# Squares of the residual shared by two engines, an earlier scaling in stick-breaking, and latent heads stacked by parity

## The chip, the core and the metric

The program runs on one core of a Trainium2 chip. It is one launch that computes two transformer layers in float32. The metric is the device time of the launch in microseconds, lower is better. The engines are named as the profile names them: PE is TensorE (matmuls; PEld its weight loads), DVE is VectorE, ACT is ScalarE, POOL is GpSimd, SP is SyncE, which here only issues DMAs. Times and starts in rows are microseconds from the start of the profiled span.

## What is computed

512 tokens, width 1024, two layers. Layer 0 mixes by eight latent heads (MLA: a query of 64 plain and 32 rotary rows per head, one rotary key shared by all heads) and eight block-attention heads (MoBA); layer 1 mixes by sixteen stick-breaking heads. Each mixing and each feed-forward part ends in a norm and is added to the residual h, and the next part starts with the norm of the new h.

```python
def mla_attention(...):                       # layer 0, heads 0..7
    q = rmsnorm(c_q) @ w_uq                   # per head: 64 plain rows, 32 rotary rows
    kv = rmsnorm(c_kv) @ w_ukv                # per head: 64 key rows, 64 value rows
    logits = (q_nope . k_nope + rope(q_rope) . rope(k_rope)) * scale   # causal softmax
def stick_breaking_attention(q, k, v):        # layer 1, 16 heads
    z = q . k * scale
    log_1m = where(strict, log_sigmoid(-z), 0)
    acc = reverse_cumsum(log_1m) - log_1m
    w = where(strict, exp(log_sigmoid(z) + acc), 0)
    return w . v
for layer in range(2):
    mixed = attention(rmsnorm(h)) @ w_out
    h = h + rmsnorm(mixed, mix_post_g)
    f = (silu(gate) * up) @ w_down            # gate, up = rmsnorm(h) @ w_gate_up
    h = h + rmsnorm(f, ffn_post_g)
```

## The kernel before

Everything is held transposed: a tile has 128 rows of the model width and 512 tokens as columns. To keep float32 accuracy each operand is split into a high part (rounded by a copy on ACT) and a low part (the difference, on DVE), and each product is three matmuls, hi x hi, lo x hi and hi x lo (`mm3`, lines 381 to 383). Weights stream through three slots of `w_raw` in chunks of 128 x 1024: SP loads a chunk when the low part of the chunk three before is done, ACT writes `w_hi` (`split_hi`, L369), DVE writes `w_lo` (`split_lo`, L376), PE uses it. The order on every engine is written out by hand; an engine takes its instructions strictly in that order and waits on semaphores, so a DVE instruction that waits holds up all that stand behind it.

**The three residual steps** (`res_dve`, `res_act`, `res_pool`, after each mixing or feed-forward part but the last) run in two halves of 256 tokens. For each of eight row tiles n, DVE writes the scaled branch to a quarter of `tf` (L647), POOL adds it to the residual (L725), ACT writes `u_hi` (L691), DVE writes `u_lo` (L657), and PE multiplies with the first three chunks of the next part, `c`, `c+1`, `c+2` (`first_products`). The splits of these chunks stand between the `u_lo` steps: the one of `c+1` behind tile 2 of the first half. Then the new h is squared on ACT (L482, two halves of eight tiles) and summed on DVE (L488, 14 adds of 128 x 256 into `sq_sum`, half after half). PE sums over rows (`stat_pe`, L411), ACT and DVE make 1/rms (L432, L437, L442), PE spreads it over the rows (`spread_pe`, L424), DVE copies it to `r_pre` (L449).

**The start of stick-breaking** (L2073 to L2093 on DVE). Projections of the pairs of heads are scaled by `r_pre` as they leave their PSUM banks (`sb_scale`, L1490), q and k of a pair are split (L1500, L1504), v is transposed on PE (L1434) and split (L1510). PE makes z for a head (`z_pe`), ACT and DVE make the softplus (`z_act_exp`, `z_dve_clamp` L1544, `z_act_ln`, `z_dve` L1555), DVE splits it (L1563, L1567), PE sums it (`c_pe`, L1579), ACT makes the stick weights (L1588), DVE and POOL split them (L1595, L1599), PE multiplies with v. The z of a pair's second head uses banks 3 to 5, in which the projections (0,2), (1,0) and (1,1) lie until DVE has scaled them. The banks' reads are counted by `qj_read`; bank 7 is used by all later projections in turn.

**The latent heads** (`layer0_items`, `item_pe`, `item_scale`, `scores_pe`). For each pair of heads PE projects q of head 0, k of head 0, q of head 1, k of head 1 and both values; a query tile has 96 rows, its last 32 are rotated on DVE and POOL (L1096, L1104, L1107, L1111), then q and k are split (ACT L1239, DVE L1286) and the scores are made with 96 contracted rows.

## Time and profile before

| | us |
|---|---|
| median of 3 runs | 1394.21 (1387.27 to 1395.02) |
| the profiled execution, its own time | 1389.55 |
| its span | 1387.5 |
| PE busy in it | 1333.9 |

The page gives busy time by engine and the chain of work that ended last; the waits view says which instruction of another engine ended an engine's idle time; the timeline gives the instructions of one engine in order of time, with the idle time ahead of each in brackets; the windows view gives busy time and the granted TensorE clock in a stretch (1.00 is 2.4 GHz, 0.50 is 1.2 GHz). The chain of waits is PE for 88% of the span, so what counts is PE's idle time, its clock, and the work that it has.

### The profile page before, as it was taken

What the parts mean: (1) busy time and instruction counts of PE and PEld (TensorE: products, weight loads), DVE (VectorE), ACT (ScalarE), POOL (GpSimd) and SP (SyncE); (2) the same over time, 40 slices, a digit from 0 to 9 for tenths busy, and PEclk for the clock granted to TensorE, in tenths of its full rate; (3) what the DMA queues carried; (4) which work ended last, traced back from release to release, by engine and by line L of the source; (5) the groups of instructions that cost most, each with busy time, mean ns of one, the idle gap of its engine ahead of it and who ended that gap; (6) DMA issues with size and microseconds to landing.
All of it is one profiled execution on the core that took longest, in us unless ns stands there. A gap on an engine that the chain in (4) does not pass through costs nothing.

```text
span 1387.5 us, 17888 instructions
## 1 busy us (share of the span) xinstructions
PE 1333.9 (96%) x6687; PEld 1122.3 (81%) x6687; DVE 730.9 (53%) x1005; ACT 543.7 (39%) x869; POOL 252.6 (18%) x185
## 2 busy tenths in 40 slices
PE   7888999999999999999988999999999999999997
PEld 5666888888888888888877888888898888888886
DVE  4777554437554544322467666765475455443223
ACT  5366665555322222222353444433553232232122
POOL 0333100033211111010231222222421111110002
PEclk9989999999999999999998999999999999999999
DMA  5311332132333333323221121120323333332321
GB/s 164 109 41 45 84 84 62 46 92 77 107 91 99 97 91 102 94 87 97 76 61 31 47 60 45 45 71 21 91 77 106 91 105 91 95 117 83 100 91 61
DMA packets 187219, 112.16 MB, mean 81 GB/s; under 512 B 8944, under 2 KB 181557, under 8 KB 187166
## 3 DMA queue, kind: packets, MB, share of 16 engines
q1 hardware_dynamic: 185356, 106.68, 26.3%
q0 software_dynamic: 640, 2.10, 0.5%
q10 hardware_dynamic: 1170, 2.66, 0.5%
q8 instruction: 35, 0.57, 0.2%
q14 instruction: 18, 0.15, 0.0%
HBM read 109.30 MB, written 4.74 MB: 82 GB/s over the span
## 4 chain that ended last, share of the span: by engine, by line
PE 88%; DVE 6%; ACT 2%; POOL 1%; issue 1%; DMA 1%; SPq 0%; POOLq 0%; DVEq 0%; ACTq 0%
PE banks L381 28%; PE banks L383 27%; PE banks L382 27%; PE banks L1579 3%; DVE w_lo L376 1%; PE banks L1373 1%; PE banks L424 1%; DVE u_lo L657 1%; DMA x_tokens<-in_x_dram 1%; ACT probsT_hi L1381 0%; DVE logits L1335 0%; PE banks L411 0%; DVE tf L1260 0%; DVE tf L647 0%; POOL rope_tmp L1104 0%
## 5 line engine op out<-in xcount | busy, mean ns | idle before, releaser
L381 PE MATMUL banks<-u_hi,w_hi 128*128 128x512 f32 (+1 forms) x1112 | 428.1, 385 | 10.0 <-DVE u_lo L657 6.5
L376 DVE TENSOR_TENSOR w_lo<-w_raw,w_hi 128x1024 fp32r<-128x1024 f32 (+2 forms) x200 | 291.9, 1463 | 272.1 <-ACT w_hi L369 271.8
L382 PE MATMUL banks<-u_lo,w_hi 128*128 128x512 f32 (+1 forms) x1112 | 421.5, 379 | 0.0
L383 PE MATMUL banks<-u_hi,w_lo 128*128 128x512 f32 (+1 forms) x1112 | 421.4, 379 | 0.0
L369 ACT ACTIVATE w_hi<-w_raw 128x1024 fp32r<-128x1024 f32 (+2 forms) x200 | 206.3, 1032 | 246.0 <-PE banks L383 246.0
L381 PEld LDWEIGHTS banks<-u_hi,w_hi 128*128 128x128 f32 x1112 | 213.0, 192 | 50.0 <-DVE u_lo L657 7.7
L383 PEld LDWEIGHTS banks<-u_hi,w_lo 128*128 128x128 f32 x1112 | 212.5, 191 | 38.9
L382 PEld LDWEIGHTS banks<-u_lo,w_hi 128*128 128x128 f32 x1112 | 212.7, 191 | 37.8 <-issue 1.0
L853 POOL TENSOR_TENSOR up<-up,gate 128x512 f32<-128x512 f32 x44 | 71.8, 1633 | 393.5 <-DVE up L877 358.5
L834 ACT ACTIVATE gate<-gate 128x512 f32<-128x512 f32 x44 | 27.9, 635 | 204.3 <-DVE gate L873 204.3
L1599 POOL TENSOR_TENSOR stick_lo<-stick,stick_hi 128x1280 fp32r<-128x1280 f32 x16 | 56.8, 3547 | 199.8 <-DVE stick_hi L1595 199.8
L381 PE MATMUL banks<-hidden_hi,w_hi 128*128 128x512 f32 (+1 forms) x198 | 73.6, 372 | 0.0
L383 PE MATMUL banks<-hidden_hi,w_lo 128*128 128x512 f32 (+1 forms) x198 | 73.4, 371 | 0.0
L382 PE MATMUL banks<-hidden_lo,w_hi 128*128 128x512 f32 (+1 forms) x198 | 73.4, 370 | 0.0
L381 PE MATMUL banks<-w_hi,hidden_hi 128*128 128x512 f32 x176 | 70.3, 399 | 0.4 <-ACT h_tokens L1044 0.3
L383 PE MATMUL banks<-w_hi,hidden_lo 128*128 128x512 f32 x176 | 69.4, 395 | 0.0
L382 PE MATMUL banks<-w_lo,hidden_hi 128*128 128x512 f32 x176 | 69.0, 392 | 0.0
L877 DVE TENSOR_TENSOR up<-banks,r_pre 128x512 f32<-128x512 f32 x44 | 30.4, 691 | 71.1 <-PE banks L383 71.1
L873 DVE TENSOR_TENSOR gate<-banks,r_pre 128x512 f32<-128x512 f32 x44 | 30.4, 691 | 69.8 <-PE banks L383 69.7
L1346 ACT ACTIVATE logits<-logits,neg_max 128x512 f32<-128x512 f32 (+1 forms) x64 | 35.3, 554 | 38.5 <-DVE neg_max L1339 38.5
L550 POOL TENSOR_TENSOR sq_sum<-sq_sum,sq_tile 128x512 f32<-128x512 f32 x14 | 18.2, 1300 | 174.6 <-ACT block_out L531 174.6
L725 POOL TENSOR_TENSOR residual<-residual,tf 128x256 f32<-128x256 f32 x42 | 41.5, 1019 | 33.9 <-DVE tf L647 33.9
(238 smaller groups left out, 2045.2 us busy)
## 6 DMA issues: line engine op xcount, KB each, us to landing
w_raw<-in_ffn_w_gate_up_dram SPq DMA_DIRECT2D x88, 512.0 KB, 3.7
w_raw<-in_ffn_w_down_dram SPq DMA_DIRECT2D x30, 512.0 KB, 3.5
w_raw<-in_sb_w_qkv_dram SPq DMA_DIRECT2D x24, 512.0 KB, 3.8
w_raw<-in_ab_w_in_dram SPq DMA_DIRECT2D x17, 512.0 KB, 3.9
w_raw<-in_ffn_w_down_dram SPq DMA_DIRECT2D x16, 448.0 KB, 3.4
w_raw<-in_ab_w_out_dram SPq DMA_DIRECT2D x8, 512.0 KB, 3.7
w_raw<-in_sb_w_out_dram SPq DMA_DIRECT2D x8, 512.0 KB, 3.7
bias_by_distance<-bias_rows ACTq DMA_DIRECT2D x1, 2560.0 KB
```

What stands on the lines that cost most here:

```text
L369: act.activation(wh[:, c.slot, 0:w], raw[:, c.slot, 0:w], ACT.Copy).then_inc(w_hi, 1)
L376: dve.tensor_tensor(wl[:, c.slot, 0:w], raw[:, c.slot, 0:w], wh[:, c.slot, 0:w].bitcast(F32), ALU.subtract).then_inc(w_lo, 1)
L381: nc.tensor.matmul(o, lh, rh, start=start, stop=False, skip_group_check=True)
L382: nc.tensor.matmul(o, lh, rl, start=False, stop=False, skip_group_check=True)
L383: return nc.tensor.matmul(o, ll, rh, start=False, stop=stop, skip_group_check=True)
L725: nc.gpsimd.tensor_tensor(hT[:, n, half(h)], hT[:, n, half(h)], quarter(n), ALU.add)\
L853: nc.gpsimd.tensor_tensor(us[:, n0 % 3, :], us[:, n0 % 3, :], gs[:, n0 % 3, :], ALU.mult)\
L873: nc.vector.tensor_tensor(gs[:, b, :], bank(2 * b), r_pre[:, :], ALU.mult).then_inc(gu_read, 1)
L877: nc.vector.tensor_tensor(us[:, b, :], bank(2 * b + 1), r_pre[:, :], ALU.mult).then_inc(gu_read, 1)
L1346: ins = act.activation(logits[:, b, at:at + w], logits[:, b, at:at + w], ACT.Exp, bias=nmx[:, b, i:i + 1], accum_out=den[:, b, i:i + 1])
L1579: mm = nc.tensor.matmul(Z[:, at:at + w], lt[:, :], n[:, COL_AT[jj]:COL_AT[jj] + w], start=False, stop=False, skip_group_check=True)
L1599: nc.gpsimd.tensor_tensor(swl[:, e, :], wf[:, :], swh[:, e, :].bitcast(F32), ALU.subtract)\
```

## The change

**Residual.** The sum of squares is shared: POOL adds the first half's seven tiles (after its residual adds), DVE the second half's; ACT squares the two halves in turn, tile by tile, and each half has two quarters of `tf` to itself. The split of chunk `c+1` on DVE comes behind tile 3 in place of tile 2. The split of `c+5` leaves the end of the residual step and comes behind `diag` and ahead of the copy to `r_pre` (on ACT behind the load of the function table). In layer 1's start PE makes the row sums inside the projection (1,0), behind its fifth row tile, where they came behind the whole of it, and the spread inside (1,1) behind its first row tile, where it came behind the fourth.

**Stick-breaking ramp.** DVE scales (1,0) and (1,1) before the clamp of head 0 and before the split of v; (1,1) goes to `diag`, since `tf` has two tiles. PE's z of head 1 waits for five bank reads in place of six. In the first pair DVE scales (1,2) ahead of two weight splits, which it used to follow.

**Latent heads.** k of both heads of a pair is one projection of 128 rows, and is split by two copies on ACT and two on DVE, one for each 64 rows. q of an odd head is a tile of 128 rows: its rotary rows are rows 32 to 63, its plain rows 64 to 127, and rows 0 to 31 hold other values that meet key rows of zero. q of an even head keeps its 96 rows above 32 rows of zero. The scores contract 128 rows. So the chunk of w_uq comes by three DMAs in place of one, the rotary table by two in place of one, the rotated key is written to both row ranges (one more POOL add at the first rotation), and POOL clears six pads at the start. The query tiles have two buffers in place of three.

```diff
@@ layer0_items
-                       ("mq", p, 1, cq, False, True), ("mk", p, 1, ck, False, False),
-                       ("mv", p, 0, ck, False, True), ("vt", p, 0, None, False, False)])
+                       ("mq", p, 1, cq, False, True), ("mv", p, 0, ck, False, True),
+                       ("vt", p, 0, None, False, False)])
@@ square_h, add_h_squares
-                before = (KD - 1) * h + n - 4
-                if before > 0:
-                    act.wait_ge(hq_added, H_ADDS * r + before)
-                dst = quarter((KD - 1) * h + n)
+                if n > 2:
+                    act.wait_ge((ha_added, hb_added)[h], (KD - 1) * r + n - 2)
+                dst = quarter(2 * h + n % 2)
...
-            nc.vector.tensor_tensor(acc[:, half(h)], acc[:, half(h)], quarter((KD - 1) * h + n), ALU.add)\
-                .then_inc(hq_added, 1)
+            op(acc[:, half(h)], acc[:, half(h)], quarter(2 * h + n % 2), ALU.add).then_inc(added, 1)
@@ res_dve
-                    if h == 0 and n == 2:
+                    if h == 0 and n == 3:
                         split_lo(dve, Chunk(c + 1))
...
-            for n in range(1, 4):
-                add_h_squares(dve, r, 0, n)
+            for n in range(1, 3):
+                add_h_squares(dve, nc.vector.tensor_tensor, r, 1, n)
             split_lo(dve, Chunk(c + 3))
-            for n in range(4, KD):
-                add_h_squares(dve, r, 0, n)
-            for n in range(1, KD):
-                add_h_squares(dve, r, 1, n)
+            for n in range(3, KD):
+                add_h_squares(dve, nc.vector.tensor_tensor, r, 1, n)
             split_lo(dve, Chunk(c + 4))
-            split_lo(dve, Chunk(c + 5))
@@ res_pool
+            for n in range(1, KD):
+                add_h_squares(pool, nc.gpsimd.tensor_tensor, r, 0, n)
@@ item_pe, item_act, item_lo
-                mm = project(pe, b[0:MLA_QH, :], c, KQ, 2 * MLA_QH, e * MLA_QH, MLA_QH, cqh, cql)
+                m = P if e else MLA_QH
+                mm = project(pe, b[0:m, :], c, KQ, 2 * MLA_QH, e * HD, m, cqh, cql)
             elif kind == "mk":
-                mm = project(pe, b[0:HD, :], c, KKV, P, e * HD, HD, ckh, ckl)
+                mm = project(pe, b, c, KKV, P, 0, P, ckh, ckl)
...
+                for rows, b in mk_dst(p):
+                    ins = act.activation(mq[2][rows, b, :], scaled_tile(it)[rows, :], ACT.Copy)
...
+                for rows, b in mk_dst(p):
+                    ins = nc.vector.tensor_tensor(mq[3][rows, b, :], scaled_tile(it)[rows, :],
+                                                  mq[2][rows, b, :].bitcast(F32), ALU.subtract)
@@ sb_pair_pe, sb_pair_dve
             if first:
-                pe.wait_ge(qj_read, 6)
+                pe.wait_ge(qj_read, 5)
...
+                if first:
+                    sb_scale(dve, p + 1, q, 2)
                 sb_split_dve(dve, p + 1, 1)
                 sb_split_dve(dve, p + 1, 2)
-                sb_scale(dve, p + 1, q, 2)
+                if not first:
+                    sb_scale(dve, p + 1, q, 2)
@@ vector, start of layer 1
-            stat_dve(dve, N_SB, 0, r_pre)
+            stat_dve(dve, N_SB, 0, None)
+            split_lo(dve, Chunk(CH_SB + 5))
+            stat_copy_dve(dve, N_SB, 0, r_pre)
...
             sb_scale(dve, 0, 0, 2)
+            sb_scale(dve, 1, 1, 0)
+            sb_scale(dve, 1, 1, 1)
             z_dve_clamp(dve, 0, 0)
             sb_item_dve(dve, 0, 0, 3)
-            sb_scale(dve, 1, 1, 0)
-            sb_scale(dve, 1, 1, 1)
@@ tensor, start of layer 1
-            sb_item_pe(pe, 1, 1, 0)
-            stat_pe(pe, N_SB, 0, (hq_added, 2 * H_ADDS))
-            sb_item_pe(pe, 1, 1, 1, lambda: spread_pe(pe, N_SB, 0))
+            def sums():
+                h_added(pe, 1)
+                stat_pe(pe, N_SB, 0, None)
+            sb_item_pe(pe, 1, 1, 0, sums, 4)
+            sb_item_pe(pe, 1, 1, 1, lambda: spread_pe(pe, N_SB, 0), 0)
```

DVE in the first half of the residual step ahead of layer 1 (`tf` is the scaled branch, `u_lo` the low part that PE waits for, `w_lo` the split of chunk `c+1`), before:

```order
L657 SCALAR_TENSOR_TENSOR u_lo<-residual,gains,u_hi 128x256
L647 SCALAR_TENSOR_TENSOR tf<-block_out,gains,banks 128x256
L376 TENSOR_TENSOR w_lo<-w_raw,w_hi 128x1024
L657 SCALAR_TENSOR_TENSOR u_lo<-residual,gains,u_hi 128x256
L647 SCALAR_TENSOR_TENSOR tf<-block_out,gains,banks 128x256
```

and now:

```order
L668 SCALAR_TENSOR_TENSOR u_lo<-residual,gains,u_hi 128x256
L658 SCALAR_TENSOR_TENSOR tf<-block_out,gains,banks 128x256
L668 SCALAR_TENSOR_TENSOR u_lo<-residual,gains,u_hi 128x256
L658 SCALAR_TENSOR_TENSOR tf<-block_out,gains,banks 128x256
L383 TENSOR_TENSOR w_lo<-w_raw,w_hi 128x1024
```

The first row of each is tile 2; tile 3 now stands ahead of the split. The other two residual steps move in the same way.

DVE at the start of layer 1, from the copy of the spread norm on (`softplus` 128x1280 is the clamp of head 0, then its log step; `tf` and `diag` are scaled projections), before:

```order
L449 COPY r_pre<-banks 128x512
L1490 SCALAR_TENSOR_TENSOR tf<-banks,r_pre 128x512 x2
L1500 TENSOR_TENSOR sb_q_lo<-tf,sb_q_hi 64x512 x2
L1504 TENSOR_TENSOR sb_k_lo<-tf,sb_k_hi 128x512
L1490 SCALAR_TENSOR_TENSOR tf<-banks,r_pre 128x512
L1544 TENSOR_SCALAR softplus<-softplus 128x1280
L1510 TENSOR_TENSOR sb_v_lo<-banks,sb_v_hi 128x4x64 x2
L1490 SCALAR_TENSOR_TENSOR tf<-banks,r_pre 128x512 x2
L1555 SCALAR_TENSOR_TENSOR softplus<-softplus,banks 128x1280
```

and now:

```order
L383 TENSOR_TENSOR w_lo<-w_raw,w_hi 128x1024
L462 COPY r_pre<-banks 128x512
L1537 SCALAR_TENSOR_TENSOR tf<-banks,r_pre 128x512 x2
L1547 TENSOR_TENSOR sb_q_lo<-tf,sb_q_hi 64x512 x2
L1551 TENSOR_TENSOR sb_k_lo<-tf,sb_k_hi 128x512
L1537 SCALAR_TENSOR_TENSOR tf<-banks,r_pre 128x512 x2
L1537 SCALAR_TENSOR_TENSOR diag<-banks,r_pre 128x512
L1591 TENSOR_SCALAR softplus<-softplus 128x1280
L1557 TENSOR_TENSOR sb_v_lo<-banks,sb_v_hi 128x4x64 x2
L1602 SCALAR_TENSOR_TENSOR softplus<-softplus,banks 128x1280
```

The scalings of (1,0) and (1,1) moved from behind the split of v to ahead of the clamp, and the split of `c+5` stands ahead of the copy.

POOL around the end of the same residual step, before:

```order
L725 TENSOR_TENSOR residual<-residual,tf 128x256 x14
L1834 MEMSET sb_v_hi 128x8x64
L1834 MEMSET sb_v_lo 128x8x64
L1839 MEMSET sb_q_hi 64x2x512 x2
L1839 MEMSET sb_q_lo 64x2x512 x2
```

and now:

```order
L729 TENSOR_TENSOR residual<-residual,tf 128x256 x14
L501 TENSOR_TENSOR sq_sum<-sq_sum,tf 128x256 x7
L1898 MEMSET sb_v_hi 128x8x64
L1898 MEMSET sb_v_lo 128x8x64
L1903 MEMSET sb_q_hi 64x2x512 x2
L1903 MEMSET sb_q_lo 64x2x512 x2
```

Seven adds stand ahead of the clears of the stick-breaking pads.

## Rows read from the trace of the kernel before

**Rows 1.** The page: busy us, share of the span and instructions by engine.
```profile
PE 1333.9 (96%) x6687; PEld 1122.3 (81%) x6687; DVE 730.9 (53%) x1005; ACT 543.7 (39%) x869; POOL 252.6 (18%) x185
```

**Rows 2.** Waits of PE: us in total, times, longest us.
```profile
PE banks L381 <- DVE mla_k_lo L1286: 9.0, 8, 2.7
PE banks L381 <- DVE u_lo L657: 6.5, 6, 1.9
```

**Rows 3.** Windows: busy us (x) of PE, PEld, DVE, ACT, POOL; PEclk, DMA, GB/s.
```profile
690.00:695.00 5.00, 5.00 (x25) 4.91 (x24) 2.83 (x6) 1.44 (x3) 0.00 (x0) 0.50 0.08 19
730.00:735.00 5.00, 5.00 (x18) 4.44 (x19) 4.89 (x6) 1.91 (x3) 0.00 (x0) 0.50 0.00 0
1006.50:1012.50 6.00, 6.00 (x28) 6.00 (x29) 3.68 (x9) 2.18 (x5) 1.37 (x2) 0.50 0.32 91
315.00:320.00 5.00, 5.00 (x31) 5.00 (x31) 3.77 (x9) 2.02 (x5) 1.21 (x2) 0.66 0.37 107
```

**Rows 4.** Timeline of DVE, third residual step: start us, us, instruction, [idle before].
```profile
1003.30 0.57 DVE L657 SCALAR_TENSOR_TENSOR u_lo<-residual,gains,u_hi 128x256 fp32r<-128x256 f32 x1
...
1004.18 1.37 DVE L376 TENSOR_TENSOR w_lo<-w_raw,w_hi 128x1024 fp32r<-128x1024 f32 x1
1005.47 0.94 DVE L657 SCALAR_TENSOR_TENSOR u_lo<-residual,gains,u_hi 128x256 fp32r<-128x256 f32 x1
```

**Rows 5.** Timeline of PE at the same place.
```profile
1006.47 0.58 PE L381 MATMUL banks<-u_hi,w_hi 128*128 128x256 f32 x1 [1.93 <-DVE u_lo L657]
...
1007.98 0.99 PE L416 MATMUL banks<-ones,sq_tile 128*128 128x1 f32 x4
...
1013.53 0.60 PE L424 MATMUL banks<-diag,ones 128*128 128x256 f32 x2
```

**Rows 6.** POOL adds of 128x256: by tile (min/median/max ns), then the timeline.
```profile
L556 POOL TENSOR_TENSOR sq_sum<-sq_sum,sq_tile x3: 740/740/927, 299.3 to 311.0; 128x256 f32<-128x256 f32 x3
...
307.62 1.84 POOL L725 TENSOR_TENSOR residual<-residual,tf 128x256 f32<-128x256 f32 x1
```

**Rows 7.** Timelines of DVE and PE, from the second residual step's squares to z.
```profile
707.57 5.52 DVE L488 TENSOR_TENSOR sq_sum<-sq_sum,tf 128x256 f32<-128x256 f32 x11
...
713.78 0.95 PE L411 MATMUL banks<-ones,sq_sum 128*128 128x1 f32 x8
...
723.49 0.47 PE L381 MATMUL banks<-sb_q_hi,sb_k_hi 128*128 128x512 f32 x1 [2.29 <-DVE sb_k_lo L1504]
```

**Rows 8.** Timelines of DVE, then PE, at the start of stick-breaking.
```profile
728.58 1.28 DVE L1490 SCALAR_TENSOR_TENSOR tf<-banks,r_pre 128x512 f32<-128x512 f32 x2
...
732.15 1.49 DVE L1567 TENSOR_TENSOR nsp_lo<-softplus,nsp_hi 128x1280 fp32r<-128x1280 f32 x1
...
747.00 5.10 DVE L376 TENSOR_TENSOR w_lo<-w_raw,w_hi 128x1024 fp32r<-128x1024 f32 x2
...
729.92 0.79 PE L381 MATMUL banks<-sb_q_hi,sb_k_hi 128*128 128x512 f32 x1 [3.60 <-DVE tf L1490]
...
740.66 0.40 PE L1579 MATMUL banks<-nsp_hi,negtri 128*128 128x512 f32 x1
...
744.97 0.47 PE L381 MATMUL banks<-sb_q_hi,sb_k_hi 128*128 128x512 f32 x1 [1.42 <-ACT stick L1588]
...
752.76 0.66 PE L1434 MATMUL banks<-ident,tf 128*128 128x128 f32 x4 [2.62 <-DVE tf L1490]
...
756.56 0.56 PE L381 MATMUL banks<-u_hi,w_hi 128*128 128x512 f32 x1
```

**Rows 9.** Timelines of PE and DVE in the latent heads.
```profile
91.79 0.44 PE L381 MATMUL banks<-ckv_hi,w_hi 128*64 128x512 f32 x1 [0.32 <-DVE tf L1260]
...
93.23 0.39 PE L381 MATMUL banks<-probsT_hi,v_hi 128*128 128x512 f32 x1
...
110.27 0.68 DVE L1286 TENSOR_TENSOR mla_k_lo<-diag,mla_k_hi 64x512 fp32r<-64x512 f32 x1
...
111.00 0.50 PE L381 MATMUL banks<-mla_k_hi,mla_q_hi 96*128 96x512 f32 x1 [1.32 <-DVE mla_k_lo L1286]
```

215 lines of the change are left out of this document (134 added, 81 removed).

## The prediction

> **What bounds the kernel now.** I read the page first: PE is busy for 1333.9 of 1387.5 us [rows 1], so some 54 us of idle time and the clock are all that can go without taking work from it. The waits view says for whom PE idles: eight times for the low part of a latent key, 9.0 us, and six times for `u_lo` in the residual steps, 6.5 us [rows 2]. The timeline of PE gives four more at the start of stick-breaking: 2.29, 3.60, 1.42 and 2.62 us [rows 7, 8]. The windows view shows what these leave behind: fully busy stretches with the granted clock at 0.50, and one of 5 us with a mean of 0.66 [rows 3], each behind such an idle time. At 0.50 (1.2 GHz in place of 2.4) PE needs about twice as long for the same matmuls. So a stall there is paid twice, and a stall of 1.32 us [rows 9] is the longest I found that left the clock at 1.00 in the attention part, while those of 1.93, 2.62 and 3.60 us were followed by 0.50.
>
> **Residual steps (three).** DVE splits chunk `c+1` (1.37 us) ahead of the fourth `u_lo`, and PE stands 1.93 us for that `u_lo` [rows 4, 5]. Now the `u_lo` comes first. In the third step it can start at 1004.2 and takes 0.6 to 0.9 us (a POOL add is in its way), so PE goes on at about 1005.0 instead of 1006.47. What is late next: PE makes the row sums, until about 1006.0, then needs the split of `c+1`, which now starts 0.9 us later than it did, behind one POOL add, and ends at about 1006.6. So of 1.93 us some 1.1 come back in smaller pieces (0.5, 0.5, 0.1) and 0.8 us is gained, three times: **2.5 us**. The rest is clock. From 1006.47 to the spread at 1013.53 PE is at 0.50 nearly throughout [rows 3, 5]: 7.1 us; at full clock the same would take about half, and the row sums, 1.0 us of tiny matmuls, do not shrink as much: 4.2, so 2.9 us. The second step is alike (0.50 in rows 3): 2.7. The first had 0.66 on average over 5 us, which is 3.4 us at 0.50: 1.5. Together 7.1 us if no step falls again. New idle pieces of 0.5 with row sums between them lie nearer to the 1.32 us that left the clock alone than to 1.93, but in one stretch of 2.5 us PE now does little, so I count two thirds: **4.7 us**. Bounds: 0 and 7.1.
>
> **The squares.** Fourteen adds on DVE, of which eleven take 5.52 us [rows 7], or 0.5 each. A POOL add takes 0.74 alone, but 1.84 where a DVE split of the same kind runs beside it [rows 6]: it waited about 1.1, the length of the split. So adds of the two engines go in turn, 0.7 + 0.3 us a pair, seven pairs and a split of 1.1: some 8.2 us against 8.2 before for fourteen adds and a split. The last add comes at about 712.8, where it came at 713.1. It is not sooner. Price in the first and third step: nothing, since PE arrives for the row sums no sooner than before; it would cost what the last add is late beyond 1 us. At the start of layer 1 PE now arrives nine matmuls earlier (9 x 0.24 = 2.1 us by rows 9), at 711.7, and waits 1.1 us for the last add. Net, row sums, spread, copy and z are 1.0 us sooner: **0.9 us**, bounds -0.5 (adds a pair of 1.3) and 2.1 (no wait). The split of `c+5`, now ahead of the copy, ends before the spread does. The pads are cleared later on POOL, behind seven adds; they are needed when q is split, and I find 1.5 us to spare.
>
> What speaks against sharing is a rule of the Trainium skill. Perfetto Trace Analysis, section Optimizing Scalar/DVE Operations, says that the two engines share a read port, so that moving work from one to the other may not help. SBUF — State Buffer says that a VectorE instruction with both inputs in SBUF and a GpSimd instruction that reads SBUF exclude each other for the whole instruction. The 1.84 us row agrees. If they ran side by side the last add would come about 2.5 us sooner, and this part would give 2.1 in place of 0.9.
>
> **Stick-breaking ramp.** z of head 1 stood 3.60 us for the scaling of (1,0) and (1,1), which sat behind clamp and v split; they now run right behind (0,2), and are done 1 us before PE arrives. The stall goes, and the half clock behind it: from 729.92 to `c_pe` at 740.66 [rows 8] PE did 24 projection matmuls (5.6 us) and a z (2.2). Next is the low softplus (start 732.15 and 1.49 us, [rows 8]), which is 0.5 us sooner without the scalings (1.28 us) ahead of it. It is ready at 733.1; PE is done with the projection at 734.2, so `c_pe` starts there: 6.5 us sooner. But now the exp of head 1 is what is late: PE waits 1.5 us for the stick weights (1.42 before) and 1.1 us for the second low softplus (none before): 5.3 us sooner. The stall of 2.62 stood behind two splits of 5.10 us, held up by POOL's long stick subtraction; the scaling of (1,2) passes them and the stall goes. The splits still stand ahead of the clamp and the v split, and the projection (2,0) needs bank 7, which that frees: a **new wait of about 3 us**. (2,0) starts at 750.3 where it started at 756.56: 6.2 us. The new wait is of the size of those that were followed by half clock (rows 3, 8: 3.0 and 1.9 us); half of it falls into the wait: 1.5. So **4.7 us**, bounds 1.5 and 8.
>
> **Latent heads.** Four projections of six matmuls go, 1.44 us each [rows 9]: 5.8 us of PE work. It is no gain by itself, since PE already stood at all eight scores for the keys. An even head's scores now wait for a second low part of 64 rows (0.6 us, the step at 110.27), and an odd head's for none: the chain is 0.6 longer, then 1.2 shorter (a copy on ACT goes as well). In the first pair nothing is gained, at half clock; over the next three I get 1.3 us at the last scores, behind which PE is never idle until layer 0's end: **1.3 us**, bounds -2.4 (four times 0.6, the odd side hidden) and 5.8. 128 rows in place of 96 cost no column. Six clears fall where POOL is idle. The added POOL add at the first rotation, less than 2 x 0.74, hides behind the norm of the keys that the next rotation waits for. w_uq by three DMAs is issued chunks ahead. I take nothing for them, at worst 2 us.
>
> **Sum.** 2.5 + 4.7 + 0.9 + 4.7 + 1.3 = 14.1 us off 1389.55: 1375.5 for the profiled execution's like. The median is 4.7 above that execution, the lowest run 2.3 below it; I add a third of the 4.7: **1377**.
>
> **Rivals.**
> (a) The clock falls in all three residual steps and stays low longer behind the new 3 us wait. For it: little PE work between 1004.5 and 1006.6. Price 4.7 + 1.5: 1383.
> (b) No step falls. 14.1 + 2.4, and 1.5 if the ramp keeps its clock: 1371 to 1373. For it: 1.32 us did nothing to it.
> (c) The waits only move: latent heads lose 2.4, the ramp gives its lower bound 1.5, the residual steps only 2.5 and the squares 0: 1.6 gained; between this and 1387 it is no change. For it: every gain here ends on another wait of DVE.
> (d) Slower: the turns of POOL and DVE. If a blocked POOL add costs its 1.84 us [rows 6] at every turn, a pair takes 2.3 in place of 1.0, and the last add is 7.5 us late. PE then stands 7.5 us at the start of layer 1 and 6.5 us at each of the two other row sums, with 3 us of half clock behind each: 29 us against 14: 1392 and more. It decides from 1.7 us a pair on. Against it: the blocker there was a split of 1024 columns, an add of 256 holds it 0.3.
> (e) The squares end sooner as meant: +1.2, inside the range.
>
> **Numbers.** Forecast (1371 to 1381 with its own bounds) 0.42; (a) 0.19; (b) 0.16; (c) 0.16; (d) 0.07. A measurement of this kernel tells about 0.5%, 7 us, from no change. Faster 0.42 + 0.19 + 0.16 = 0.77, within 0.16, slower 0.07. The range 1367 to 1389 leaves out (d), most of (c) and little below.
>
> **What would show it.** In the profile after: the wait for `u_lo` at the fourth tile below 0.7 us and a wait for `w_lo` of 0.5 behind the row sums; PEclk 1.00 after at least two of three; no wait of PE for the scalings in the ramp, but one of 3 us for bank 7 at (2,0); squares that end when they ended, POOL's adds near 1.0 us each; key waits in the latent heads longer in total than 9.0. Wrong I would be if PE stands for the squares in the first or third step, or if half clock appears where there was none.

## The result, and the profile after

| | before | changed |
|---|---|---|
| median of 6 runs each, same session, us | 1391.72 (1386.03 to 1395.69) | 1374.76 (1374.26 to 1377.74) |
| the profiled execution, its own time | 1389.55 | 1374.53 |
| its span | 1387.5 | 1372.8 |
| PE busy | 1333.9 | 1321.9 |

The ratio is 0.9886, with a 95% interval of 0.986 to 0.9911: faster by 1.1%. Forecast were 1377.0 and 1367 to 1389; for the profiled execution's like 1375.5, where it took 1374.53.

The page's first row, which answers to [rows 1], and the waits of PE, which answer to [rows 2]:

```profile
PE 1321.9 (96%) x6663; PEld 1115.1 (81%) x6663; DVE 730.3 (53%) x980; ACT 543.8 (40%) x869; POOL 275.8 (20%) x213
```
```profile
PE banks L388 <- DVE mla_k_lo L1315: 12.3, 4, 4.9
...
PE banks L388 <- DVE w_lo L383: 5.5, 6, 3.5
PE banks L388 <- DVE mla_q_lo L1320: 4.8, 3, 2.3
PE banks L388 <- DVE sb_v_lo L1557: 3.4, 2, 3.2
...
PE banks L388 <- DVE u_lo L668: 1.5, 6, 0.3
```

PE has 12.0 us less of busy time: 5.0 in the three residual steps and 4.3 between z and projection (2,0), where the same matmuls now run with less half clock or none, and 2.7 in the latent heads. There 24 projection matmuls are gone, 5.8 us of work, but some of the rest has fallen to half clock (see below). The wait for `u_lo` fell from 6.5 to 1.5, the wait for keys rose from 9.0 to 12.3 and a wait for queries came in, and there is a new wait for `sb_v_lo`, which is bank 7 at projection (2,0).

The timeline of PE in the third residual step, where [rows 4, 5] stood, and its granted clock there (windows view of PE alone: length, PE busy (x), PEclk, DMA share, GB/s):

```profile
992.59 0.39 PE L388 MATMUL banks<-u_hi,w_hi 128*128 128x256 f32 x1 [0.21 <-DVE u_lo L668]
993.46 0.39 PE L388 MATMUL banks<-u_hi,w_hi 128*128 128x256 f32 x1 [0.25 <-DVE u_lo L668]
995.14 0.38 PE L388 MATMUL banks<-u_hi,w_hi 128*128 128x256 f32 x1 [0.28 <-DVE w_lo L383]
...
998.11 0.59 PE L437 MATMUL banks<-diag,ones 128*128 128x256 f32 x2
```
```profile
995.00:996.00 1.00, 0.86 (x7) 1.00 0.00 0
996.00:997.00 1.00, 1.00 (x11) 1.00 0.45 120
```

The first of these idle times, 0.21 us, was there before. The one of 1.93 us became two of 0.25 and 0.28, and the clock stays at 1.00, where it stood at 0.50 for 6 us.

The timeline of PE at the start of stick-breaking, which answers to [rows 7, 8]:

```profile
708.54 1.02 PE L424 MATMUL banks<-ones,sq_sum 128*128 128x1 f32 x8 [0.59 <-DVE sq_sum L501]
...
718.49 0.47 PE L388 MATMUL banks<-sb_q_hi,sb_k_hi 128*128 128x512 f32 x1 [0.24 <-DVE sb_k_lo L1551]
...
729.32 0.40 PE L1626 MATMUL banks<-nsp_hi,negtri 128*128 128x512 f32 x1
...
733.62 0.47 PE L388 MATMUL banks<-sb_q_hi,sb_k_hi 128*128 128x512 f32 x1 [1.42 <-ACT stick L1635]
...
736.87 0.50 PE L1626 MATMUL banks<-nsp_hi,negtri 128*128 128x512 f32 x1 [0.85 <-DVE nsp_lo L1614]
...
745.36 0.49 PE L388 MATMUL banks<-u_hi,w_hi 128*128 128x512 f32 x1 [3.19 <-DVE sb_v_lo L1557]
```

The waits of 3.60 and 2.62 us for scalings are gone, and one of 3.19 has come at the start of (2,0).

**All runs by stage.** The next table cuts each trace at starts of PE's rows: the first spread of the program (35.35 before), the first product of a residual step (311.03), its spread (320.52), the row sums of layer 1 (713.78), z (723.49), `c_pe` (740.66), projection (2,0) (756.56), and so on. Heads: first spread to first product of step 1. Steps: first product to spread. Sums: spread of step 2 to row sums. z, c, (2,0): each from the one ahead. Rest: (2,0) to step 3. From the spread of step 1 to step 2 it is 363.3 in all of them. The median is of the timed runs, with that of before in the same session behind it. One of the eleven executions of only_split_moved took 2202.82 us at a granted clock of 0.555, and is left out of the ratio given below; the median of the other ten is 1383.77.

| kernel | median (before) | heads | step 1 | step 2 | sums | z | c | (2,0) | rest | step 3 |
|---|---|---|---|---|---|---|---|---|---|---|
| before | | 275.68 | 9.49 | 10.65 | 19.26 | 9.71 | 17.17 | 15.90 | 246.28 | 10.69 |
| changed | 1374.76 (1391.72) | 277.24 | 8.25 | 6.76 | 17.55 | 9.95 | 10.83 | 16.04 | 246.15 | 6.60 |
| after_again | 1375.98 (1393.62) | 277.19 | 8.24 | 6.73 | 17.56 | 9.94 | 10.82 | 16.03 | 246.12 | 6.67 |
| only_split_moved | 1383.98 (1394.15) | 275.92 | 6.76 | 8.24 | 18.85 | 9.70 | 16.72 | 16.02 | 246.10 | 6.60 |
| split_in_two | 1384.74 (1393.96) | 278.29 | 10.52 | 8.95 | 18.86 | 9.70 | 16.79 | 16.02 | 245.95 | 7.37 |
| latent_as_before | 1375.36 (1394.15) | 275.96 | 6.75 | 8.24 | 17.55 | 9.93 | 10.81 | 16.03 | 247.58 | 6.67 |
| key_halves_apart | 1376.48 (1393.96) | 276.31 | 6.75 | 8.26 | 17.55 | 9.95 | 10.81 | 16.04 | 248.89 | 6.67 |
| ramp_as_before | 1380.64 (1394.15) | 277.19 | 8.26 | 8.23 | 17.56 | 9.95 | 15.60 | 15.55 | 246.18 | 6.60 |
| squares_on_dve | 1377.78 (1394.15) | 277.28 | 8.25 | 6.74 | 16.81 | 9.88 | 10.87 | 16.01 | 249.63 | 6.60 |
| sums_as_before | 1379.07 (1393.62) | 277.32 | 8.25 | 6.74 | 18.86 | 9.81 | 12.37 | 16.05 | 248.89 | 6.66 |
| weight_splits_late | 1374.47 (1393.96) | 277.26 | 6.76 | 6.75 | 17.55 | 9.94 | 10.81 | 14.83 | 247.77 | 6.63 |
| three_mended | 1375.29 (1393.96) | 276.32 | 6.75 | 8.25 | 16.81 | 9.87 | 10.82 | 14.81 | 248.50 | 6.61 |
| v_split_first | 1374.51 (1393.62) | 277.32 | 6.77 | 6.73 | 17.55 | 9.96 | 10.81 | 12.93 | 246.52 | 6.67 |
| best | 1369.56 (1393.62) | 278.32 | 8.15 | 8.25 | 16.82 | 9.87 | 10.82 | 12.92 | 246.60 | 6.66 |

The span of the changed kernel is 14.7 shorter, and by stage: heads +1.56, steps -1.24, -3.89 and -4.09, from the second spread to z -1.47, from z to (2,0) -6.20, rest -0.13, and +0.72 behind step 3. This last part is not PE's: its last matmul comes 365.6 us behind the third spread in both traces. From that matmul's end to the end of the span it takes 7.92 or 7.93 us in the five kernels with the latent heads as before, and 8.44 to 8.75 in the nine with the stacked ones. SP issues the last store 5.31 us behind the start of the last matmul before and 5.66 in the changed kernel, although POOL's add ahead of it starts 3.47 us behind that matmul in both. So this 0.7 us goes with the stacked heads too; why is not shown.

Up to the first spread PE has the same work in all these kernels, and it took 35.35 to 37.67 us (35.39 and 36.86 in the two traces of the changed program); so stages are compared, not spans.

### The profile page after: what moved, and what is told of

Its sections match the earlier page's. It is cut to its first block, busy times and chain, and to the rows that moved or that the text cites. A ratio compares the mean times of both kernels' runs of the same rounds, so it can differ in the third digit from the quotient of the medians.

```text
span 1372.8 us, 17850 instructions
## 1 busy us (share of the span) xinstructions
PE 1321.9 (96%) x6663; PEld 1115.1 (81%) x6663; DVE 730.3 (53%) x980; ACT 543.8 (40%) x869; POOL 275.8 (20%) x213
## 4 chain that ended last, share of the span: by engine, by line
PE 86%; DVE 7%; ACT 3%; POOL 2%; issue 1%; DMA 0%; POOLq 0%; ACTq 0%; SPq 0%; DVEq 0%
PE banks L388 27%; PE banks L390 27%; PE banks L389 27%; PE banks L1626 3%; DVE w_lo L383 1%; PE banks L1409 1%; DVE u_lo L668 1%; DVE tf L658 1%; PE banks L437 1%; DVE logits L1371 0%; POOL rope_tmp L1118 0%; POOL residual L729 0%; DVE probsT_lo L1421 0%; ACT w_hi L376 0%; DVE diag L455 0%
## 5 line engine op out<-in xcount | busy, mean ns | idle before, releaser
L388 PEld LDWEIGHTS banks<-u_hi,w_hi 128*128 128x128 f32 x1112 | 210.1, 189 | 49.6 <-issue 8.2
```

Source lines behind the costliest of these rows:

```text
L388: nc.tensor.matmul(o, lh, rh, start=start, stop=False, skip_group_check=True)
```

## The experiments

**What the moved split does (only_split_moved).** The kernel before with the one line of the residual steps:

```diff
-                    if h == 0 and n == 2:
+                    if h == 0 and n == 3:
                         split_lo(dve, Chunk(c + 1))
```

> The kernel before with one line changed: in the three residual steps the split of chunk c+1 stands behind tile 3 in place of tile 2. Theory 1 (stall and clock): the steps, measured from the first product to the spread, fall from 9.49, 10.65 and 10.69 us to 8.2, 6.8 and 6.6 as in the changed kernel: 9.2 us off, 1382.5, granted clock 1.00 behind the second and third. Theory 2 (the clock depends on other work that the change took away, such as DVE's share): only the stalls of 1.9 shrink, 2.5 us off, 1389, and the clock is at 0.50 behind all three. I hold theory 1.

The three steps took 6.76, 8.24 and 6.60 us, 9.2 less together than before, which is the whole of theory 1, and the median is some 10 below that of before (ratio 0.9934, interval 0.9912 to 0.9957, from runs that scatter by 6 to 10 us on both sides). The whole change brought 17 to 18 between medians, so this one line is worth more than all the rest of it. But the clock did not do quite as in the changed kernel: it held in the first step and fell in the second.

**Between the two (split_in_two).** The kernel before, the split in two parts of 512 columns, behind tiles 2 and 3:

```diff
-                    if h == 0 and n == 2:
-                        split_lo(dve, Chunk(c + 1))
+                    if h == 0 and n in (2, 3):
+                        split_lo_part(dve, Chunk(c + 1), n - 2)
```

> The kernel before, with the split of chunk c+1 in the three residual steps cut in two parts of 512 columns: one behind tile 2, where it stood, and one behind tile 3. PE's wait for the fourth u_lo becomes about 1.2 us (1.93 less half of a split of 1.37), between the 1.93 of before and the 0.27 of the changed kernel. Theory 1 (the half clock follows from how long PE stands): with 1.2 it comes in some of the steps; a step takes 7.5 without it and 9.5 with it; 1385 to 1390. Theory 2 (any idle piece at this place drops the clock): all three at 0.50, 9.5 to 10.5 us each, 1391. Theory 3 (under the 1.32 us that left the clock alone in the latent heads): none, 7.5 each, 1385.

PE stood 0.26 or 0.27 and then 1.38 us in each step, a little more than the 1.2 of the expectation. The timeline of PE in step 1, and the clock behind it (windows as above):

```profile
316.71 0.39 PE L389 MATMUL banks<-u_hi,w_hi 128*128 128x256 f32 x1 [0.27 <-DVE u_lo L665]
318.72 0.39 PE L389 MATMUL banks<-u_hi,w_hi 128*128 128x256 f32 x1 [1.38 <-DVE u_lo L665]
```
```profile
320.00:322.00 2.00, 2.00 (x10) 0.50 0.38 109
```

Step 1 had 0.50 (10.52 us), step 2 a part of it (8.95), step 3 none (7.37): theory 1. Theory 2 falls by step 3, and theory 3 by step 1. This is one trace, of the slowest of five executions (1388.85); the median of 1384.74 would fit theory 3 as well. And since PE stood equally long in all three steps, the length of the wait alone does not settle the clock. Nor are the 1.32 us that left it alone in [rows 9] a safe length. In this same trace the same wait ahead of head 6, with one of 0.81 us some 2.5 us later, was followed by half clock (timeline and windows of PE), and so it was in the trace of best; both have heads of 278.3. Before, waits of 1.30 and 0.91 us at this place left the clock at 1.00.

```profile
136.25 0.50 PE L389 MATMUL banks<-mla_k_hi,mla_q_hi 96*128 96x512 f32 x1 [1.32 <-DVE mla_k_lo L1294]
```
```profile
138.00:148.00 10.00, 9.19 (x41) 0.66 0.00 0
```

**Latent heads undone (latent_as_before).** The changed kernel with the latent heads, their DMAs, pads and rotation as they were; of the diff:

```diff
-                       ("mq", p, 1, cq, False, True), ("mv", p, 0, ck, False, True),
-                       ("vt", p, 0, None, False, False)])
+                       ("mq", p, 1, cq, False, True), ("mk", p, 1, ck, False, False),
+                       ("mv", p, 0, ck, False, True), ("vt", p, 0, None, False, False)])
...
-                mm = project(pe, b, c, KKV, P, 0, P, ckh, ckl)
+                mm = project(pe, b[0:HD, :], c, KKV, P, e * HD, HD, ckh, ckl)
```

> The changed kernel with the latent heads as they were (two projections for k, 96-row queries, one DMA for w_uq); the residual steps and the ramp stay changed. Two theories. (1) By my prediction's term the stacked latent heads give 1.3 us: this kernel would take 1376 (1.3 above the 1374.8 of the changed one), the first residual product would start 1.3 us later than the 312.6 of the changed trace. (2) By the start times in the two traces (311.03 before, 312.63 after, for the first product of the first residual step) the stacking costs 1.6 us: 1373.2, first residual product at 311.0, and the four low key waits of 12.3 us fall back to eight of about 9.0. I hold (2).

The median did not fall to 1373.2: it is 1375.36, the same as that of the changed kernel within their scatter. By stage theory (2) holds: the heads take 275.96 against 277.24, 1.3 less, and the low key waits are eight of 9.0 us in total again. The end is 0.7 shorter too (7.93 in place of 8.67). In this trace that is taken back by half clock behind the wait at (2,0) (rest 247.58), and steps 1 and 2 only change places. Starts of the scores, from the first spread, tell more: 33.56 us for head 0 before, 33.56 here and 34.96 changed; from head 0 to head 7 it is 75.29 us before, 75.56 here and 75.29 changed. So in the heads the loss is at the first scores, and behind them the stacking neither gains nor loses.

**Why the first scores are late (key_halves_apart).** The two halves of a key are signalled apart on ACT and DVE:

```diff
-                for rows, b in mk_dst(p):
-                    ins = act.activation(mq[2][rows, b, :], scaled_tile(it)[rows, :], ACT.Copy)
-                ins.then_inc(pj_hi, 1)
+                for (rows, b), done in zip(mk_dst(p), (ke_hi, pj_hi)):
+                    act.activation(mq[2][rows, b, :], scaled_tile(it)[rows, :], ACT.Copy).then_inc(done, 1)
```

> The changed kernel, but the even and the odd half of a stacked key projection are signalled apart: DVE subtracts the even half as soon as ACT has copied it, and PE starts the even head's scores behind that. In the changed trace ACT copies both halves (1.25 us) before DVE begins, and DVE then subtracts both (1.39) before PE goes on; the first scores start at 70.35 against 68.91 before. Theory 1 (this chain of two copies and two subtractions is what the stacking costs): the first scores start 1.2 to 1.4 us sooner, those of the other even heads too, and from the first spread (35.4) to the first residual product it takes 273.5 to 276 in place of 277.2: 1371 to 1373.5. Theory 2 (something else, such as the extra POOL add at the first rotation, holds the first scores): no more than 0.3 us, 1374.5.

The changed kernel first, then this one (timelines of ACT, DVE and PE):

```profile
67.63 1.25 ACT L1258 ACTIVATE mla_k_hi<-tf 64x512 fp32r<-64x512 f32 x2
...
68.91 1.39 DVE L1315 TENSOR_TENSOR mla_k_lo<-tf,mla_k_hi 64x512 fp32r<-64x512 f32 x2 [0.56 <-ACT mla_k_hi L1258]
...
70.35 0.80 PE L388 MATMUL banks<-mla_k_hi,mla_q_hi 128*128 128x512 f32 x1 [4.94 <-DVE mla_k_lo L1315]
```
```profile
68.39 1.40 DVE L1318 TENSOR_TENSOR mla_k_lo<-tf,mla_k_hi 64x512 fp32r<-64x512 f32 x2
69.13 0.80 PE L389 MATMUL banks<-mla_k_hi,mla_q_hi 128*128 128x512 f32 x1 [3.60 <-DVE mla_k_lo L1318]
```

DVE no longer stands 0.56 for the second copy, and PE goes on behind the first subtraction: the first scores come 33.64 us behind the first spread, within 0.1 of before, and those of heads 2, 4 and 6 come 1.2 to 2.1 us sooner than in the changed kernel. Theory 1 holds for the cause. But the odd heads now wait about 1.8 us each for their query, and the heads as a whole take 276.31, 0.3 over the upper end of what I gave, and still 0.6 over before. The median, 1376.48, is no better than the changed kernel's; its trace has 2.7 us of half clock behind (2,0).

**The ramp undone (ramp_as_before).** The changed kernel with DVE's order at the start of stick-breaking as it was:

```diff
-                pe.wait_ge(qj_read, 5)
+                pe.wait_ge(qj_read, 6)
...
-            sb_scale(dve, 1, 1, 0)
-            sb_scale(dve, 1, 1, 1)
             z_dve_clamp(dve, 0, 0)
             sb_item_dve(dve, 0, 0, 3)
+            sb_scale(dve, 1, 1, 0)
+            sb_scale(dve, 1, 1, 1)
```

and the scaling of (1,2) behind two weight splits again.

> The changed kernel with the stick-breaking ramp as it was (scalings of (1,0) and (1,1) behind clamp and v split, two weight splits ahead of the scaling of (1,2), z of head 1 waits for six bank reads). Theory 1: the ramp's new order is worth what the traces show from the start of z (0,0) to that of projection (2,0), 33.07 before and 26.87 after: 6.2 us, so 1381.0, with waits of 3.6 and 2.6 us back and the granted clock at 0.50 behind the 3.6. Theory 2: the half clock in the ramp came from the whole of what PE did since the half clock of the second residual step, which is gone now; then the stalls return and the clock stays at 1.00: about 5.1 us of half clock less, 1377. I hold theory 1, two to one.

```profile
726.62 0.80 PE L388 MATMUL banks<-sb_q_hi,sb_k_hi 128*128 128x512 f32 x1 [3.60 <-DVE tf L1527]
...
747.88 0.66 PE L1471 MATMUL banks<-ident,tf 128*128 128x128 f32 x4 [2.61 <-DVE tf L1527]
...
751.34 0.49 PE L388 MATMUL banks<-u_hi,w_hi 128*128 128x512 f32 x1 [0.94 <-DVE sb_v_lo L1547]
```
```profile
726.00:728.00 2.00, 1.38 (x3) 0.56 0.00 0
728.00:730.00 2.00, 2.00 (x10) 0.58 0.00 0
730.00:732.00 2.00, 2.00 (x14) 1.00 0.00 0
```

1380.64, where theory 1 gave 1381.0: both waits are back. From z to (2,0) it took 31.15 us, 4.3 over the changed kernel and 1.9 under before, since half clock lasted some 4 us in place of 7. So in this trace the truth lies between the two theories, and that the median meets theory 1 is in part luck: 1.5 of the 6.0 us that its span has over the changed kernel's lie in step 2, where the clock fell.

**The new wait at (2,0) (weight_splits_late, then v_split_first).** First both weight splits of the first pair behind the split of v:

```diff
-                sb_split_dve(dve, p + 1, 1)
-                sb_split_dve(dve, p + 1, 2)
                 z_dve_clamp(dve, p + 1, 0)
                 sb_item_dve(dve, p + 1, q, 3)
+                sb_split_dve(dve, p + 1, 1)
+                sb_split_dve(dve, p + 1, 2)
```

> The changed kernel with the two weight splits of the first stick-breaking pair moved behind the clamp of pair 1 and the split of its v. Theory 1 (the two splits, 4.51 us from 737.33, are what the new wait of 3.19 us for bank 7 at (2,0) stands behind): the wait goes, (2,0) starts at 742.2 in place of 745.36, 3.2 us off: 1371.6, and the runs scatter less, since no half clock can follow that wait. Theory 2 (the wait moves on, to the load of the next chunks, which these splits release 4 us later): a wait for w_lo of 1 to 3 us at (2,1) or (2,2), 1373 to 1375.

```profile
741.27 0.76 DVE L1557 TENSOR_TENSOR sb_v_lo<-banks,sb_v_hi 128x256 fp32r<-128x256 f32 x2 [1.88 <-ACT sb_v_hi L1506]
741.95 2.35 DVE L383 TENSOR_TENSOR w_lo<-w_raw,w_hi 128x1024 fp32r<-128x1024 f32 x2
```
```profile
743.22 0.50 PE L388 MATMUL banks<-u_hi,w_hi 128*128 128x512 f32 x1 [1.96 <-DVE w_lo L383]
```

The wait did move on, as in theory 2, though to the split itself and not to a load: the first of the two is the weight of (2,0). It gained 1.2 us, and 1.6 of half clock behind it took that back. Next, only the second split late, and ACT copies v ahead of the log step:

```diff
                 sb_split_dve(dve, p + 1, 1)
-                sb_split_dve(dve, p + 1, 2)
                 z_dve_clamp(dve, p + 1, 0)
                 sb_item_dve(dve, p + 1, q, 3)
+                sb_split_dve(dve, p + 1, 2)
@@ ACT
                 z_act_exp(act, p + 1, 0)
+                sb_item_act(act, p + 1, q, 3)
                 z_act_ln(act, p + 1, 0)
-                sb_item_act(act, p + 1, q, 3)
```

> The changed kernel; in the first stick-breaking pair only the weight split of chunk (2,0) stays ahead of the clamp, the other goes behind the split of v, and ACT copies v ahead of the log step. With both splits late PE waited 1.96 us for w_lo of (2,0) in place of 3.19 for v. If the order of the two splits and of v is the whole cause: the split of (2,0) is done at about 739, v at about 741, PE comes at 742.2 and does not wait: 3.2 us off and no half clock behind it: 1371 to 1372, from c_pe to (2,0) 12.8 us in place of 16.04. If POOL's long subtraction holds the first split as long as it held both (4.5 us): a wait of 1 to 2 us stays, 1374.

```profile
738.17 3.38 DVE L383 TENSOR_TENSOR w_lo<-w_raw,w_hi 128x1024 fp32r<-128x1024 f32 x1
741.47 0.81 DVE L1591 TENSOR_SCALAR softplus<-softplus 128x1280 f32<-128x1280 f32 x1
742.20 0.74 DVE L1557 TENSOR_TENSOR sb_v_lo<-banks,sb_v_hi 128x256 fp32r<-128x256 f32 x2
742.87 1.21 DVE L383 TENSOR_TENSOR w_lo<-w_raw,w_hi 128x1024 fp32r<-128x1024 f32 x1
```
```profile
743.08 0.49 PE L388 MATMUL banks<-u_hi,w_hi 128*128 128x512 f32 x1
```

The wait is gone, and the stage takes 12.93 where 12.8 was expected. POOL's long subtraction holds one split for 3.38 us, and the one behind it takes 1.21. The median is 1374.51 against 1375.98 for the changed kernel on the same chip, its lowest run 1372.11 against 1374.30; about half of the 3.1 us shows in the timed runs.

**The squares (squares_on_dve).** The changed kernel, all fourteen adds on DVE, the halves in turn:

```diff
-            for n in range(1, 3):
-                add_h_squares(dve, nc.vector.tensor_tensor, r, 1, n)
+            for n in range(1, 3):
+                for h in range(2):
+                    add_h_squares(dve, nc.vector.tensor_tensor, r, h, n)
```

> The changed kernel with all fourteen square adds on DVE again (order by tile, both halves in turn), POOL makes none; ACT's order, the places of the splits and of the row sums stay changed. Theory 1 (the two engines exclude each other, so sharing does not end sooner): fourteen adds and one split take DVE 8.2 us from 701.0 on, end 709.2 against 708.4, so row sums of layer 1 at 709.3 against 708.54: 0.8 us slower there, and nothing in the other steps, 1375.5. Theory 2 (sharing halves the time as meant, 2.5 us sooner): 2.5 us slower, 1377.3. Theory 3 (sharing costs): the adds of POOL and DVE block each other, DVE alone ends sooner: 1373.5 to 1374.

The changed kernel's DVE and POOL, then this kernel's DVE, in the second step:

```profile
703.73 3.62 DVE L501 TENSOR_TENSOR sq_sum<-sq_sum,tf 128x256 f32<-128x256 f32 x4
```
```profile
702.94 4.13 POOL L501 TENSOR_TENSOR sq_sum<-sq_sum,tf 128x256 f32<-128x256 f32 x4 [0.55 <-ACT tf L494]
```
```profile
704.95 2.76 DVE L501 TENSOR_TENSOR sq_sum<-sq_sum,tf 128x256 f32<-128x256 f32 x8
```

Side by side four pairs take 4.13 us, the first of them drawn out by a weight split on DVE (POOL's add took 1.47 us there and 0.74 to 0.75 in the other three); the undisturbed pairs start 0.89 us apart. DVE alone does eight adds in 2.76, or 0.69 for two. From the second spread to the row sums it is 16.81 us against 17.55: theory 3, sharing costs 0.7. The median, 1377.78, says the opposite. In its trace what was gained is lost behind (2,0), at half clock (rest 249.63 in place of 246.15), a place that this edit doesn't touch. That the timed runs, all at 1376.42 and more, lost it there too is not shown.

**Where the row sums stand (sums_as_before).** The changed kernel, squares still shared:

```diff
-            sb_item_pe(pe, 1, 1, 0, sums, 4)
-            sb_item_pe(pe, 1, 1, 1, lambda: spread_pe(pe, N_SB, 0), 0)
+            sb_item_pe(pe, 1, 1, 0)
+            sums()
+            sb_item_pe(pe, 1, 1, 1, lambda: spread_pe(pe, N_SB, 0))
```

> The changed kernel with the row sums of layer 1 behind the whole of projection (1,0) and the spread behind the fourth row tile of (1,1), as before; the squares stay shared. Theory 1 (the row sums' place is what gains at the start of layer 1, since the last square comes at 708.5, 0.6 us after PE): row sums at 710.1, spread about 1.5 us later than now, z at 720.0 in place of 718.5: 1376. Theory 2 (the shared squares gain it): nothing is lost, 1374.5.

```profile
721.55 0.47 PE L388 MATMUL banks<-sb_q_hi,sb_k_hi 128*128 128x512 f32 x1 [2.39 <-DVE sb_k_lo L1551]
```
```profile
723.00:725.00 2.00, 2.00 (x10) 0.50 0.03 8
```

From the second spread to z it takes 28.67 us, 1.17 more than in the changed kernel, and PE's wait ahead of z is 2.39 as it was before (2.29). It is followed by half clock, 1.5 us more up to `c_pe`. So of the 1.47 us gained at the start of layer 1, 1.2 come from the place of the row sums: theory 1. But the early place needs early squares. The last add ends 17.41 us behind the second spread in all the kernels with shared squares, 18.16 in only_split_moved, which has DVE's old order, and 16.67 with DVE alone and the halves in turn. With the last add at 18.16 PE would have stood 0.75 longer at the early place, and moving the row sums alone would have given about 0.5; this is an estimate from these times, no run has it. The median is 3.1 above the changed kernel's, twice what I gave: I had priced no half clock, and this trace has some behind the wait for z and more behind (2,0) (rest 248.89).

**The program once more, and a better one (after_again, three_mended, best).**

> The changed kernel itself, once more, on the same chip as the three that follow. What it tells: whether its first residual step (8.25 us in its first trace, clock at 0.50 behind three idle pieces of 0.27) and the wait of 3.19 us at (2,0) (clock 1.00 in its first trace, about 0.50 in five other traces of kernels with this wait or one of 2 us) come out the same for the same program. Theory 1 (the clock at such places is not settled by the instructions, and differs from run to run): at least one of the three steps or the ramp differs by 1.5 us from the first trace; median 1374.5 to 1376. Theory 2 (it is settled by the program): all stages within 0.1 us of the first trace.

For these two traces it is theory 2: all stages agree within 0.07 us, although the start took 1.5 us longer. But weight_splits_late and v_split_first run the same instructions up to 735 us, and had 6.76 and 6.77 in step 1, where the changed kernel had 8.25 and 8.24. So it is theory 1 after all: the instructions do not settle the clock there. The timed runs of the one program lie between 1374.30 and 1377.41.

> The changed kernel with three edits: key halves signalled apart, weight splits of the first pair late, all squares on DVE (from the second spread to the row sums of layer 1: 16.8 us in place of 17.55 in the run that had the squares on DVE alone). If they add up: 1374.8 less 2.5, less 3.2, less 0.7: 1368.4. If the squares on DVE bring back a cost of their own elsewhere, as the 1377.8 of that run might say (3.0 above the changed kernel; its trace lost them to half clock behind the 3.2 us wait, which this kernel has not): 1371.

The median is 1375.29, neither of the two. In its trace heads, sums and (2,0) gained 0.9, 0.7 and 1.2 us, and the rest lost 2.4 behind the wait of 1.96 for w_lo, which stays as in weight_splits_late.

> Latent heads as before, all squares on DVE, the ramp as in v_split_first, the rest as in the changed kernel. By stages of the traces: 275.9 for the latent heads (277.2 changed), 16.8 from the second spread to the row sums (17.55), 12.8 from c_pe to (2,0) (16.04): 1.3 + 0.7 + 3.2 = 5.2 us off the changed kernel, 1369.5, if none of the gains is taken back by half clock in the first or second step (1.5 each).

1369.56 (1368.97 to 1374.65, ratio to before 0.985, interval 0.9821 to 0.9879), 6.4 below the changed kernel on the same chip, where 5.2 was expected; 0.8 that I had not counted is the end, 7.92 in place of 8.72. It has the latent heads as before, squares on DVE, the row sums early, the moved scalings, and one weight split behind v. Three runs are within 1369.6, two at 1374.6 with a granted clock of 0.987 in place of 0.992; the profiled one is of the latter kind, with 2.4 us lost in the latent heads (278.32 in place of 275.9) and both first steps at 8.2. No single edit gained more than 1.5 us between medians, and squares_on_dve lost 3, where the four together gained 6. In the traces the difference is the half clock of other stages.

## Why the prediction was right, step by step

**Residual steps.** Forecast 2.5 for the stalls and 4.7 for the clock, 7.2; measured 1.24 + 3.89 + 4.09 = 9.2, of which 4.2 are stalls and 5.0 the clock. The stalls were under-sized: the wait for `u_lo` fell from 6.5 to 1.5 and that for `w_lo` rose from 4.6 to 5.5, 1.4 us less per step in place of 0.8, since the new idle times are two of 0.25 to 0.28 and not 0.5, 0.5 and 0.1. The clock came out as counted, in two steps of three, but the ground for that count does not stand. It placed the new waits nearer to 1.32 us, the longest that had left the clock alone in the attention part, than to 1.93. At the start of layer 1, in the same trace of before, the wait of 2.29 us ahead of z [rows 7] was followed by this (windows of PE alone):

```profile
724.00:726.00 2.00, 2.00 (x18) 1.00 0.03 8
```

The length of the wait did not tell the two apart there, nor in split_in_two, and the two thirds were a guess that came out. Over the twelve traces with the split behind tile 3, a step took 6.6 to 6.8 us in 24 of 36 cases and 8.2 in the others, which is two thirds. What I did not see is that it goes by place: step 3 held in all twelve, steps 1 and 2 in six each.

**Squares.** Forecast: a pair of adds 1.0 us, the last add no sooner, PE waits 1.1 for it, and 0.9 gained at z by the place of the row sums. Measured: 0.89 us for an undisturbed pair, 1.03 on average with the one that a split held up, the last add 17.4 us behind the second spread where it was 18.6, a wait of 0.59, and 1.47. Some 0.4 us of the last two differences is the clock behind the second residual step: only_split_moved, with squares and row sums as before, has its last add at 18.16 and takes 28.55 us from that spread to z, where before takes 28.97. So "the last add no sooner" was wrong by 0.75, and the edits of this part gave 1.05, where 0.9 was forecast. The rivals (d), turns of 2.3 us, and (e), squares in half the time, are both out. What I had not seen is that DVE could do the same work faster than its 0.5 per add in [rows 7], so that sharing is a loss of 0.7 and not nothing. The Trainium skill (SBUF — State Buffer, section Who interferes with whom) says that a VectorE instruction with two inputs in SBUF contends with a GpSimd instruction that reads SBUF. The trace agrees: a DVE add took 0.78 us beside POOL's and 0.42 alone. That one holds up the other for its whole length is seen in a long pair (the split of 3.38 us in v_split_first). The adds do not show it: their pairs start 0.89 us apart, less than the 0.42 and 0.74 that the two last by themselves.

**Ramp.** Forecast 6.2 from z to (2,0), less 1.5 for half clock behind a new wait of 3 us: 4.7. Measured 6.20, and a wait of 3.19 at the place named, behind the splits named. The half clock didn't come in the changed kernel. It came in four of the six traces that have this wait, at 1.4 to 3.5 us, so the term had its price, and that both traces of the changed program were spared it is luck. The waits of 1.5 and 1.1 us were 1.42 and 0.85.

**Latent heads.** Here the sign was wrong: 1.3 gained was forecast, 1.3 to 1.6 are lost. The steps that failed are "in the first pair nothing is gained" and the 1.3 us "over the next three". I added 0.6 us to the even heads' chain for a second subtraction, and left out the second copy on ACT, which DVE waits for: both together make 1.4 (first scores 34.96 us behind the first spread in place of 33.56). Nor did the later pairs give anything: from the first scores to the last it takes 75.29 us in both, so what bounds them is not PE's work. My lower bound, -2.4, holds it, even with the 0.7 us at the end of the program.

Half clock also came in the heads where there was none, which I had named as a sign of being wrong: behind the waits for the keys of heads 2 and 6, 2.33 and 2.50 us in place of 0.16 and 1.30. Windows of PE around head 2, before and changed:

```profile
88.00:98.00 10.00, 9.53 (x54) 1.00 0.00 0
```
```profile
88.00:98.00 10.00, 7.67 (x34) 0.83 0.00 0
```

It is not what cost the gain. In key_halves_apart the clock is 1.00 over the same stretch and around head 6, and from the first scores to the last it takes 75.59.

**Sum.** 14.1 was forecast for the profiled execution, and 15.0 measured. The latent heads were 2.9 too good; steps, start of layer 1 and ramp were too low by 2.0, 0.6 and 1.5. These errors nearly cancel, which is luck; with the 0.7 lost at the end of the program, in no term of mine, they leave 14.7 us of span.

**The median.** That before's profiled execution was a quick one is borne out: in three more sessions its median was 1393.6 to 1394.2, with runs at a granted clock of 0.978 to 0.981 at 1393.4 to 1395.8 and runs at 0.983 to 0.986 at 1386 to 1390. But the changed kernel's profiled execution was not quick in the same way: its median is 1374.76 and its own time 1374.53, so the 1.5 us that I added for the median were not there. The changed kernel's lie within 3.5 us, at 0.988 to 0.991. So the change is worth 15 us between the profiled executions and 17 to 18 between medians, and it also takes most of the scatter away.

## What to carry to other kernels

Look first at what an in-order engine does ahead of the instruction that the matmuls wait for: one weight split moved behind one `u_lo` gave 10 of some 17 us. Taking work from an engine that always waits for another gives nothing, and splitting an instruction in two lengthens the chain by the producer's half too, if it signals once. Where half clock follows an idle time, price the wait with and without it, and judge an edit by its own stage in the trace, since the clock of another stage can outweigh it in the median.

## What I had not expected of the hardware

**PE's timeline does not tell the clock.** The changed kernel and latent_as_before run the same instructions in step 1, with the same idle times to 0.02 us. PE's timeline and the windows of each, the changed kernel first:

```profile
316.42 0.39 PE L388 MATMUL banks<-u_hi,w_hi 128*128 128x256 f32 x1 [0.26 <-DVE w_lo L383]
```
```profile
316.00:317.00 1.00, 0.74 (x6) 0.96 0.00 0
317.00:318.00 1.00, 1.00 (x7) 0.50 0.20 58
318.00:319.00 1.00, 1.00 (x7) 0.50 0.99 263
```
```profile
316.45 0.39 PE L382 MATMUL banks<-u_hi,w_hi 128*128 128x256 f32 x1 [0.27 <-DVE w_lo L377]
```
```profile
316.00:317.00 1.00, 0.73 (x6) 1.00 0.00 0
317.00:318.00 1.00, 1.00 (x11) 1.00 0.15 35
318.00:319.00 1.00, 1.00 (x11) 1.00 0.98 274
```

0.50 in one and 1.00 in the other, 1.5 us apart at the spread. In the same way a wait of 3.2 us at (2,0) left the clock at 1.00 in two traces (both of the changed program) and was followed by 0.50 in four. The 24 to 12 above was made up of such cases. What settles it stays open; it is not the instructions, since v_split_first, which differs from the changed kernel only from 735 us on, had 1.00 in step 1. The Trainium skill (TensorE: Matmul & The Clock Gate, section What's actually happening) says that what the chip watches runs freely and does not restart with the kernel, so that at its start the same kernel can come out differently. It says so of a kernel's start; in its middle these traces agree as far as they go: the two of the changed program took 8.25 and 8.24 us in step 1, v_split_first 6.77.

**Alternating accumulators.** Eleven adds into one half of `sq_sum` after the other took 5.52 us on DVE, 0.50 each [rows 7]. Eight adds that go to the two halves in turn took 2.76, 0.35 each. One add lasts 0.42 us in both; they start 0.53 apart in the one and 0.34 in the other. In the trace before, the single change of half among those eleven, at 709.49, also comes 0.34 behind the add ahead. So an add into the other half can start sooner. Whether it is the accumulator or the semaphore that holds the next add into the same half was not tried by itself: the program makes each wait for the one ahead in its half.

**A blocked split.** In v_split_first a split of 1024 columns took 3.38 us beside POOL's subtraction of 1280 columns (738.17), and the next one, behind it, 1.21. The subtraction ends at 740.46 and the blocked split 1.1 us later, about the length of a split.
